# Banded attention with sinks: one turned block of reciprocals in place of two spreading products, and the value product behind the next unit's turns

## What is computed

```python
def sink_softmax(s, sink):
    sk = sink.astype(jnp.float32)[:, :, None, None]
    m = jnp.maximum(jnp.max(s, axis=-1, keepdims=True), sk)
    e = jnp.exp(s - m)
    return e / (jnp.sum(e, axis=-1, keepdims=True) + jnp.exp(sk - m))
...
        p = sink_softmax(jnp.concatenate([s_band, s_ctx], axis=-1), sink_g)
        vv = jnp.concatenate([vb, vc], axis=1)
        return jnp.einsum('bkgqj,bjkd->bqkgd', p.astype(v.dtype), vv)
```

## Time and profile before

| | us |
|---|---|
| median of 3 runs | 1777.29 (1775.32 to 1777.40) |
| the profiled execution | 1775.55 |
| its span in the trace | 1773.8 |
| TensorE busy with matmuls | 1727.9 (97% of the span) |
| VectorE busy | 1213.6 (68%) |
| ScalarE busy | 808.0 (46%) |
| GpSimd busy | 782.9 (44%) |

### The profile page before, as it was taken

One profiled execution on the slowest core, in us unless ns is written; L12 is line 12 of the kernel. 1 busy time (PEld: TensorE's weight loads), 2 busy tenths in 40 slices (PEclk: granted clock), 3 DMA queues, 4 the chain that ended last, 5 costly groups with the idle time before them and its releaser, 6 DMA issues. The chain is left out here.

```text
span 1773.8 us, 26025 instructions
## 1 busy us (share of the span) xinstructions
PE 1727.9 (97%) x9276; PEld 1448.6 (82%) x9276; DVE 1213.6 (68%) x1650; ACT 808.0 (46%) x1609; POOL 782.9 (44%) x540
## 2 busy tenths in 40 slices
PE   8999999999998999989999999899999999999998
PEld 6997888888887999777788878678888888888887
DVE  3628688879948999677733366875666566575767
ACT  3434333434637888656620145633333333344453
POOL 0407577766533898521122232465555555400000
PEclk9999999999999999999999999999999999999999
DMA  9233234435777665412034242233223323386734
GB/s 349 86 109 137 96 119 161 163 128 190 261 188 192 170 146 151 137 33 72 1 143 160 90 166 84 83 107 119 95 95 127 121 95 128 115 277 208 254 104 178
DMA packets 98569, 249.89 MB, mean 141 GB/s; under 512 B 12321, under 2 KB 26017, under 8 KB 98338
## 3 DMA queue, kind: packets, MB, share of 16 engines
q1 hardware_dynamic: 98466, 248.52, 42.1%
HBM read 183.07 MB, written 65.41 MB: 140 GB/s over the span
## 5 line engine op out<-in xcount | busy, mean ns | idle before, releaser
L750 POOL TENSOR_TENSOR ring<-raw_w,ring 128x512 fp32r<-128x512 f32 x120 | 187.1, 1577 | 137.0 <-ACT ring L621 137.0
L78 PE MATMUL psum<-h_hi,ring 128*128 128x512 f32 x400 | 155.9, 390 | 2.6 <-ACT z L667 2.0
L80 PE MATMUL psum<-h_hi,ring 128*128 128x512 f32 x400 | 155.6, 389 | 0.0
L79 PE MATMUL psum<-h_lo,ring 128*128 128x512 f32 x400 | 155.6, 389 | 0.0
L78 PE MATMUL psum<-u_slot 128*128 128x512 f32 x308 | 120.4, 391 | 0.8 <-DVE u_slot L2977 0.6
L80 PE MATMUL psum<-u_slot 128*128 128x512 f32 x308 | 120.1, 390 | 0.0
L79 PE MATMUL psum<-u_slot 128*128 128x512 f32 x308 | 119.9, 389 | 0.0
L621 ACT ACTIVATE ring<-raw_w 128x512 fp32r<-128x512 f32 x120 | 72.5, 625 | 100.5 <-DVE raw_w L915 35.3
L1406 DVE TENSOR_REDUCE mx<-psum 128x1 f32<-128x1280 f32 x64 | 95.2, 1487 | 8.1 <-PE psum L1292 7.4
L1339 ACT ACTIVATE e<-psum,neg_m 128x1280 f32<-128x1280 f32 x64 | 85.1, 1329 | 31.9 <-DVE neg_m L1407 31.9
L2576 POOL TENSOR_TENSOR cut_lo<-i_raw,cut_hi 128x512 fp32r<-128x512 f32 x44 | 66.8, 1520 | 59.2 <-ACT cut_hi L2431 59.2
(11 more groups left out here) (416 smaller groups left out, 5202.5 us busy)
## 6 DMA issues: line engine op xcount, KB each, us to landing
raw_w<-in_w_pairs SPq DMA_DIRECT2D x40, 512.0 KB, 5.0
qk_dram<-room SPq DMA_DIRECT2D x26, 512.0 KB, 3.6
room<-in_w_ada SPq DMA_DIRECT2D x24, 512.0 KB, 5.9
gates_dram<-ost SPq DMA_DIRECT2D x24, 512.0 KB, 3.1
b_g<-gates_dram SPq DMA_DIRECT2D x8, 1536.0 KB, 7.5
stage<-in_w_ff SPq DMA_DIRECT2D x22, 512.0 KB, 5.9
i_raw<-in_w_ff SPq DMA_DIRECT2D x22, 512.0 KB, 4.8
f_dram<-h SPq DMA_DIRECT2D x22, 512.0 KB, 3.4
```

The source lines that it names most:

```text
L78: pe.matmul(out, sh, mh, start=first, stop=False, skip_group_check=onto)
L79: pe.matmul(out, sh, ml, start=False, stop=False, skip_group_check=onto)
L80: return pe.matmul(out, sl, mh, start=False, stop=last, skip_group_check=onto)
L750: pool.tensor_tensor(w_lo[i], source(p, i), w_hi[i].bitcast(F32), ALU.subtract).then_inc(w_lo_ready, 1)
```

## The change

Each unit's two reciprocals are now written by VectorE as a 128x128 block (64 columns for each head), in the last slot of the unit's buffer of transposed weights (`spread(u)`, now a view and no product). TensorE transposes that block as one more block of the unit's third group, and ScalarE copies the third group out, so that the slot then holds the reciprocals by column. VectorE's `output` multiplies the value product into the same slot, where `output_hi` and `output_lo` read it; `y_full`, `wrec` and the two spreading products are gone. `reciprocals(u)` waits until `output_lo(u-2)` has read the slot. On TensorE `products(i-2)` stands behind `turn(i-1)`, in the program and in the ring; on VectorE group 1's copy stands ahead of `output`, and `output_lo` of units 0 to 8 ahead of `reciprocals`; on GpSimd `output_lo` stands ahead of `sinks`. Every unit now has three groups.

```diff
@@ -1465,13 +1465,12 @@
-        pt1 = sb("wpt1", [P, 2, KEYS // P, P])
-        y_full = [sb(f"wy{b}", [P, P]) for b in range(2)]
-        mx, neg_m, sums, es, rec = (sb("wmx", [P, 2]), sb("wneg_m", [P, 2, 2]), sb("wsums", [P, 2, 2]), sb("wes", [P, 2, 2]),
-                                    sb("wrec", [P, 4, 2]))
+        pt1 = sb("wpt1", [P, 2 * KEYS // P + 1, P])
+        sb("wgap", [P, 80])
+        mx, neg_m, sums, es = (sb("wmx", [P, 2]), sb("wneg_m", [P, 2, 2]), sb("wsums", [P, 2, 2]), sb("wes", [P, 2, 2]))
...
@@ -1508,18 +1507,18 @@
-        def squares(u):
-
-            todo = [(s, k) for s in range(2) for k in range(len(tiles_of(u)))]
-            return [todo[n:n + 4] for n in range(0, len(todo), 4)]
-
-        def weights_at(u):
-
-            return pt[u % 2][:].rearrange("p s k n -> p (s k) n")
+        def blocks(u):
+
+            todo = [(s, k) for s in range(2) for k in range(len(tiles_of(u)))] + [None]
+            return [todo[0:4], todo[4:8], todo[8:]]
         def group(u, part):
-            return weights_at(u)[:, 4 * part:4 * part + len(squares(u)[part]), :]
+            return pt[u % 2][:, 4 * part:4 * part + len(blocks(u)[part]), :]
+
+        def spread(u):
+
...
@@ -1527,12 +1526,11 @@
+            if 0 <= i - 1 < UN:
+                for part in range(3):
+                    ring["turn", i - 1, part] = len(ring)
             if 0 <= i - 2 < UN:
                 ring["av", i - 2, 0] = len(ring)
-            if 0 <= i - 1 < UN:
-                for part in range(len(squares(i - 1))):
-                    ring["turn", i - 1, part] = len(ring)
-                ring["rec", i - 1, 0] = len(ring)
             if i in POOL_STEPS:
                 ring["pool", POOL_STEPS.index(i), 0] = len(ring)
...
@@ -1645,35 +1643,32 @@
             def turn(u):
-                for part, todo in enumerate(squares(u)):
+                for part, todo in enumerate(blocks(u)):
                     b, bank = use("turn", u, part)
-                    for s in sorted({s for s, _ in todo}):
-                        pe.wait_ge(exp_done[s], u + 2)
-                    for n, (s, k) in enumerate(todo):
-                        mm = pe.transpose(bank[:, n * P:(n + 1) * P], e[u % 2][s][:, k * P:(k + 1) * P], ident[:])
+                    for n, block in enumerate(todo):
+                        if block is None:
+                            pe.wait_ge(rec_ready, u + 1)
+                            src = spread(u)
+                        else:
+                            s, k = block
+                            pe.wait_ge(exp_done[s], u + 2)
+                            src = e[u % 2][s][:, k * P:(k + 1) * P]
+                        mm = pe.transpose(bank[:, n * P:(n + 1) * P], src, ident[:])
                     mm.then_inc(turned[b], 1)
             def products(u):
                 kv = at(u)[0]
                 if u % KU == 0:
                     pe.wait_ge((v_in, v1_in)[kv], 16 * 2)
-                for part in range(len(squares(u))):
+                for part in range(3):
                     b, used = slot("turn", u, part)
                     pe.wait_ge(free[b], used + 2)
...
-                mm.then_inc(turned[b], 1)
-
-            def spread(u):
-                pe.wait_ge(rec_ready, u + 1)
-                b, bank = use("rec", u)
-                for s in range(2):
-                    mm = pe.matmul(bank[s * HD:(s + 1) * HD, 0:P], rec[:, u % 4, s:s + 1].to_broadcast([P, HD]), ident[:],
-                                   start=True, stop=True)
...
@@ -1729,7 +1722,8 @@
                 if 0 <= i - 1 < UN:
                     turn(i - 1)
-                    spread(i - 1)
+                if 0 <= i - 2 < UN:
+                    products(i - 2)
...
@@ -1763,22 +1757,13 @@
-                act.activation(out, banks[4 + b][:, 0:len(squares(u)[part]) * P].rearrange("p (k n) -> p k n", n=P), ACT.Copy)\
+                act.activation(out, banks[4 + b][:, 0:len(blocks(u)[part]) * P].rearrange("p (k n) -> p k n", n=P), ACT.Copy)\
...
-            def over_copy(u):
-                b, used = slot("rec", u)
-                if u == 0:
-                    act.wait_ge(*att["squares"])
-                if u >= 2:
-                    act.wait_ge(yc_lo_ready, u - 1)
-                act.wait_ge(turned[b], used + 1)
-                act.activation(y_full[u % 2][:], banks[4 + b][:, 0:P], ACT.Copy).then_inc(free[b], 1)
...
@@ -1826,6 +1809,7 @@
                 if 0 <= i - 1 < UN:
                     copy_out(i - 1, 0)
+                    copy_out(i - 1, 2)
                 if 0 <= i - 2 < UN:
...
@@ -1882,9 +1866,9 @@
             for u in range(POOL_FROM, UN):
-                sinks(pool, u)
                 if u - 3 >= POOL_FROM:
                     output_lo(pool, u - 3)
+                sinks(pool, u)
...
@@ -1912,12 +1896,15 @@
                 ch.link(v.tensor_tensor(sums[:, u % 2, :], sums[:, u % 2, :], es[:, u % 2, :], ALU.add))
-                v.reciprocal(rec[:, u % 4, :], sums[:, u % 2, :]).then_inc(rec_ready, 1)
+                if u >= 2:
+                    v.wait_ge(yc_lo_ready, u - 1)
+                v.reciprocal(spread(u).rearrange("p (s d) -> p s d", s=2), sums[:, u % 2, :].unsqueeze(2).to_broadcast([P, 2, HD]))\
+                 .then_inc(rec_ready, 1)
...
@@ -1925,8 +1912,9 @@
                 v.wait_ge(turned[b], used + 1)
-                v.wait_ge(*final("rec", u))
-                v.tensor_tensor(y_full[u % 2][:], banks[4 + b][:, 0:P], y_full[u % 2][:], ALU.mult).then_inc(free[b], 1)
+                b2, used2 = slot("turn", u, 2)
+                v.wait_ge(free[b2], used2 + 2)
+                v.tensor_tensor(spread(u), banks[4 + b][:, 0:P], spread(u), ALU.mult).then_inc(free[b], 1)
...
@@ -1960,6 +1948,8 @@
                 if i < UN:
                     maximum(ch, i, 0)
+                if 0 <= i - 3 < POOL_FROM:
+                    output_lo(v, i - 3)
                 if 0 <= i - 1 < UN:
                     reciprocals(ch, i - 1)
...
@@ -1973,13 +1963,10 @@
                     da_lo(DA_STEPS.index(i - 1))
                 if i - 1 in POOL_STEPS:
                     pool_lo(POOL_STEPS.index(i - 1))
-                if 0 <= i - 3 < POOL_FROM:
-                    output_lo(v, i - 3)
+                if 0 <= i - 1 < UN:
+                    copy_out(i - 1, 1)
                 if 0 <= i - 2 < UN:
                     output(i - 2)
-                if 0 <= i - 1 < UN:
-                    for part in range(1, len(squares(i - 1))):
-                        copy_out(i - 1, part)
...
```

More of the change, by code:

```diff
@@ L1467, in window @@
         on = [sb(f"on{j}", [P, 4, P]) for j in range(2)]
-        pt1 = sb("wpt1", [P, 2, KEYS // P, P])
-        y_full = [sb(f"wy{b}", [P, P]) for b in range(2)]
-        mx, neg_m, sums, es, rec = (sb("wmx", [P, 2]), sb("wneg_m", [P, 2, 2]), sb("wsums", [P, 2, 2]), sb("wes", [P, 2, 2]),
-                                    sb("wrec", [P, 4, 2]))
+        pt1 = sb("wpt1", [P, 2 * KEYS // P + 1, P])
+        sb("wgap", [P, 80])
+        mx, neg_m, sums, es = (sb("wmx", [P, 2]), sb("wneg_m", [P, 2, 2]), sb("wsums", [P, 2, 2]), sb("wes", [P, 2, 2]))
         val = [sb("wval", [P, TT, HD])[:], keep["wa_val1"][:]]
         e = [[sb(f"we{b}{s}", [P, KEYS]) for s in range(2)] for b in range(2)]
-        pt = [sb("wpt0", [P, 2, KEYS // P, P]), pt1]
+        pt = [sb("wpt0", [P, 2 * KEYS // P + 1, P]), pt1]
         kc1 = keep["wa_kc1"]
@@ L1509, in tiles_of @@
             return [0, 1] + [2 + b for b in range(max(blk - 1, 0), min(blk + 2, TL))]
-        def squares(u):
-            todo = [(s, k) for s in range(2) for k in range(len(tiles_of(u)))]
-            return [todo[n:n + 4] for n in range(0, len(todo), 4)]
-        def weights_at(u):
-            return pt[u % 2][:].rearrange("p s k n -> p (s k) n")
+        def blocks(u):
+            todo = [(s, k) for s in range(2) for k in range(len(tiles_of(u)))] + [None]
+            return [todo[0:4], todo[4:8], todo[8:]]
         def group(u, part):
-            return weights_at(u)[:, 4 * part:4 * part + len(squares(u)[part]), :]
+            return pt[u % 2][:, 4 * part:4 * part + len(blocks(u)[part]), :]
+        def spread(u):
+            return pt[u % 2][:, 2 * len(tiles_of(u)), :]
         STEPS = UN + 3
@@ L1666, in products @@
                     for s in range(2):
-                        mm = pe.matmul(out[s * HD:(s + 1) * HD, :], val[kv][:, k, :], weights_at(u)[:, s * len(tiles) + n, :],
+                        mm = pe.matmul(out[s * HD:(s + 1) * HD, :], val[kv][:, k, :], pt[u % 2][:, s * len(tiles) + n, :],
                                        start=(n == 0), stop=(n == len(tiles) - 1))
-                mm.then_inc(turned[b], 1)
-            def spread(u):
-                pe.wait_ge(rec_ready, u + 1)
-                b, bank = use("rec", u)
-                for s in range(2):
-                    mm = pe.matmul(bank[s * HD:(s + 1) * HD, 0:P], rec[:, u % 4, s:s + 1].to_broadcast([P, HD]), ident[:],
```

(13 more changed lines are left out.)

## The result

The changed kernel takes **1819.63 us** (median; 1817.67 to 1819.69 in 4 runs) against 1777.35 (1775.32 to 1777.62 in 4 runs) for the kernel before beside it: ratio 1.0231, 95% interval 1.022 to 1.0243, 42 us slower. The profiled execution has a span of 1817.8 us with a mean clock of 0.988, before 1773.8 and 0.996.

The account below looks back on a forecast made before the run. TensorE, busy 97% of the span, was taken as the bound, with waits on VectorE's chain. 1775.55 + 26.0 (steps 8 to 31) + 6.3 (steps 1 to 7) = 1807.9 profiled, 1809 on the median; range 1795 to 1824.

Parts of the forecast that it names:

- The reciprocal at 953 ns: VectorE's 128x128 reciprocal, taken from a line through 2, 16 and 32 elements: 953 ns, +0.79 us in the chain.
- Which bank the value product takes, and who frees it: Value product waits for the low part's bank, starting 4.14 us after T, the start of head 0's mask product.
- The steps: T to T in steps 8 to 31: with turn_da +0.79 us, with pool product +1.18, with neither +1.28.
- the third kind: Steps like 23, without turn_da or pool product: value product waits for the low part's bank, 6.06 against 4.78 us.
- the 26.0: Added us over steps 8 to 31: 3.25 for three steps, taken eight times, end units left in.
- Steps 1 to 7, 6.3 us: Early steps, with GpSimd's long rows delaying VectorE's additions in steps 5 and 6: 6.3 us more, bounds 3 and 9.
- my lower bound: Early steps cost only 3 us, where VectorE's addition L1914 slips in between GpSimd's two long rows.
- The old wait that I set against step 6: TensorE's 2.27 us wait at 754.57, expected to go, in step 6's net cost of 1.7 us.
- The rest of the span, 0: End of the stage has no scores, so nothing to hide behind or pay: 0; rest of the span as before.
- The clock, the term that was short: Rival: TensorE's idle pieces drop its clock in every second step of 24, 20 us more, 1829; chance 0.09.
- The ring's new order alone would do this: Rival of a short reciprocal (282 ns): steps cost +0.60, +0.50, +0.11, giving 1790 us from the new order; chance 0.07.

Follow-up runs that it names:

- the kernel with filled waits: Changed kernel with transposes of the identity in TensorE's waits, 4 ahead of the block of reciprocals and 11 behind its wait before a low part: 1811.73 us, ratio 1.0194.
- the first experiment: Kernel before with two more linked 128x34 reciprocals into scratch between VectorE's two maxima, nothing else changed: 1799.84 us, ratio 1.0119.

## Why the prediction was right, and where it was short

1. **The reciprocal at 953 ns**: exact, from a line drawn four times beyond its last point.
2. **Which bank the value product takes, and who frees it**: right. It waited for `y_lo` in two steps of three and started at T + 4.18 (predicted 4.14); the move of the low part took that wait away.
3. **The steps**: 6.07 / 6.79 / 6.24 against 6.11 / 6.75 / 6.06. Without the end of a fall in it the third kind is 6.10. From T(8) to T(31) the kernel with filled waits takes 143.3 - 116.7 = 26.6 us more than before, where these 23 steps have 24.8 in my sum (the 26.0 less step 31); 1.6 of the 1.8 over it lie in steps 15 to 18, the short ones of units with fewer keys (4.23 to 4.81 before), which I had left in at the price of the full ones: step 18 cost 1.67 where I had 0.79.
4. **Steps 1 to 7, 6.3 us**: the size was near, 8.0 measured, but not the places. Step 5 was to bring 2.9 and brought 1.8; step 4, 1.2, brought 3.7; step 7, which shared 0.5 with steps 1 to 3, brought 2.8; step 6 was to bring 1.7 and became 0.6 shorter. In step 5 the sum of L1914 (now L1898) did not meet GpSimd's second row: it ran at 755.79 in 0.15 us, between the two rows, which was my lower bound and not my value; it did so again in step 6 (766.08). The old wait that I set against step 6 (754.57) lies in step 5; step 6 has one like it (763.05, 2.25 us). And 2.35 - 0.5 + 0.79 is 2.6, not 2.9. Falls of the clock lie in steps 4, 5 and 7 (749.0, 759.3, 776.3), and in the filled kernel step 7 was as short as before. So the near sum is luck in part: too much for GpSimd's rows, nothing for the clock. How the rest divides stays open.
5. **The rest of the span, 0**: +2.9 behind T(31), of which some 1.2 is the last of my 24 steps, so 1.7 over; one of the falls (933.3) lies there.
6. **The clock, the term that was short.** I gave it a chance of 0.09 as a case with twelve falls and 20 us, and had "one or two falls" in my range and none in my sum. Nine came in the stage, and from T(8) to T(31) five of them took 6.4 us. My argument against, that a wait of 2.27 us in step 5 was followed by no fall in that step, was one place, and the changed kernel waits 0.4 to 1.4 us in every step for 200 us. Between the profiled executions the sum was 32.3 us and the difference 44.0: of the 11.7 between them the clock from T(8) to T(31) has 6.4, the short steps 1.8, steps 1 to 7 1.7, and what lies behind T(31) 1.7.
7. **The cause, as told in the rivals, was too narrow.** "The ring's new order alone would do this", at 1790 us, does not stand. The old kernel in the new order took 1818.67, and its waits show the bank use that it has more: the product waits for group 0's copy, the spreading products for the low part. The changed kernel with a short reciprocal took 1800.39. For this one I had 282 ns where reciprocal and copy together take 0.40, and its steps came some 0.2 longer than my 5.43 / 6.07 / 5.38. And I read the long reciprocal as the cause because it was the new operation on the chain. The tables say otherwise: with the product first it costs 8 us, of which the block pays 7, and the change of order costs 42. My sum was right since it went by the end of the chain in the new order; it did not ask what the product had been hiding.

The rule that reciprocals repeat on VectorE (the Trainium skill, "VectorE: DVE Perf Modes", the walkthrough of the 8-slice pipeline, its hardware budget) is borne out in kind and not in size. The 953 ns for 128 elements are 6.2 ns more an element, as in the earlier trace rows, where the copy L1920 takes 1.06 (685 and 414 ns for 512 and 256 elements in the kernel before); they are not the 8.3 of the estimate that I had from that page.

## What to carry to other kernels

A block of work that waits for nothing new (here the value product of the unit before, 1.24 us) is the cover of the chain that runs meanwhile on other engines; before moving it behind that chain, write down what it hides and what then stands in the open. In a ring of banks, an order is two orders: list for each use which use it follows in its bank and when that one is read out, because one use more or less in a step changes every pair. And two edits whose costs cancel (two products and a bank use saved, a longer operation on the chain) look like one that does nothing: shorten the one and keep the other. Last, compare such kernels over the steady steps too: whole times also hold falls of the clock and other engines' rows, which made equal costs look like 19 and 8 us.

## What the runs showed of the hardware that I had not expected

TensorE's granted clock fell to the 1.2 GHz level, 3.4 us at a time, five times between 780 and 900 us, where the longest wait of TensorE in a piece was 1.6 us. With those waits filled by transposes it did not fall once in the same steps, and with the product first it did not fall there either. From T(8) to T(31) it fell twice in the kernel with the order alone (1818.67) and twice with the low part ahead (1808.77), once with the short reciprocal (1800.39), and not at all in the first experiment (1799.84), which waited up to 1.2 us in a piece, twice in three steps. What in the waits brings a fall was not tried.

Windows of the changed kernel from T(8) to T(31), and of the kernel with the product first and the long reciprocal from step 9 to T(31):

```profile
779.00:928.00 149.00, 111.56 (x967) 96.89 (x967) 97.80 (x204) 77.00 (x199) 20.24 (x48) 0.94 0.08 26
```

```profile
780.00:889.00 109.00, 94.99 (x900) 81.73 (x898) 88.45 (x188) 69.56 (x187) 19.66 (x48) 1.00 0.10 34
```
